# Two layers of a streaming encoder on one core: three tiles turned by a diagonal, one residual and the first ropes moved

## What is computed

```python
def trunk_layer(x, c, pos, w_ada, b_ada, g_pre, w_in, w_out, g_post, past):
    mod = jax.nn.silu(c) @ w_ada + b_ada
    shift, scale, gate = jnp.split(mod, 3, axis=-1)
    h = rms_norm(x, g_pre) * (1.0 + scale[:, None, :]) + shift[:, None, :]
    q_a, k_a, v_a, gate_a, q_i, k_i, w_i, q_b, k_b, v_b, gate_b = split_cols(h @ w_in)
    # rope on q_a, k_a, q_i, k_i, q_b, k_b
    o_a = dsa_attention(q_a, q_i, w_i, pos, k_all, v_all, ki_all)   # keys chosen by an index score, top 256
    o_b, s_new = retention(q_b, k_b, v_b, s0)
    o_b = head_group_norm(o_b).reshape(B, T, W_B).astype(x.dtype)
    mixed = jnp.concatenate([o_a * jax.nn.silu(gate_a), o_b * jax.nn.silu(gate_b)], axis=-1)
    y = rms_norm(mixed @ w_out, g_post)
    x = x + gate[:, None, :] * y
    return x, (k_a, v_a, k_i, s_new.astype(x.dtype))
```

## Time and profile before

| what | value |
|---|---|
| median of three runs | 1457.58 us (1457.34 to 1458.71) |
| the profiled execution | 1458.35 us |
| its span, first to last instruction | 1456.5 us |
| mean granted clock of TensorE | 0.992 of full speed |
| TensorE busy | 1391.7 us (96%) |
| VectorE busy | 1012.3 us (70%) |
| ScalarE busy | 790.7 us (54%) |
| GpSimd busy | 414.3 us (28%) |

### The profile page before, as it was taken

The page is one execution under the profiler, slowest core; times in us unless marked ns, Lnnn a source line. Parts: engine busy times, 40 slices in busy tenths (PEclk is TensorE's granted clock), DMA queues, the critical chain, the costliest instruction groups (busy, mean ns, idle before and its releaser), DMA issues.

```text
span 1456.5 us, 24555 instructions
## 1 busy us (share of the span) xinstructions
PE 1391.7 (96%) x7663; PEld 1064.9 (73%) x7663; DVE 1012.3 (70%) x2985; ACT 790.7 (54%) x1934; POOL 414.3 (28%) x378
## 2 busy tenths in 40 slices
PE   6989999999999999999997999999999999999996
PEld 2765777788887677668876577878788766766885
DVE  0586889999996555542397889999999655554125
ACT  2555666666315666664453566666631566666432
POOL 3750333433331011001387114433343200100100
PEclk9999999999999999999998999999999999999998
DMA  8734343212232112223252111211222211222324
GB/s 292 232 113 126 94 126 108 66 37 61 57 89 64 43 38 68 80 64 103 95 185 52 27 46 37 64 32 50 61 56 77 68 37 48 71 64 67 109 87 159
DMA packets 125190, 122.05 MB, mean 84 GB/s; under 512 B 33256, under 2 KB 94024, under 8 KB 125064
## 3 DMA queue, kind: packets, MB, share of 16 engines
q1 hardware_dynamic: 124608, 120.36, 27.6%
q10 hardware_dynamic: 456, 0.13, 0.0%
HBM read 93.55 MB, written 26.90 MB: 83 GB/s over the span
## 4 chain that ended last, share of the span: by engine, by line
PE 63%; DVE 27%; issue 4%; DMA 2%; ACT 2%; POOL 1%; DVEq 0%; ACTq 0%; SPq 0%; POOLq 0%
PE proj L969 12%; PE proj L970 12%; PE proj L972 11%; PE turn L948 10%; DVE U L1712 7%; PE logit L996 6%; PE out_bank L1023 5%; PE spare L996 2%; DVE U L1897 2%; DVE probsT_more L1785 1%; DVE probsT_more L1787 1%; DVE by_cos_sin L1656 1%; DVE turned L1667 1%; DVE by_cos_sin L1654 1%; PE spare L934 1%
## 5 line engine op out<-in xcount | busy, mean ns | idle before, releaser
L969 PE MATMUL proj<-w_hi,h_hi 128*128 128x512 f32 (+2 forms) x1440 | 576.8, 401 | 2.6 <-ACT U L1266 1.5
L970 PE MATMUL proj<-w_lo,h_hi 128*128 128x512 f32 (+2 forms) x1440 | 537.1, 373 | 0.0
L972 PE MATMUL proj<-w_hi,h_lo 128*128 128x512 f32 (+2 forms) x1280 | 479.2, 374 | 0.0
L1496 POOL TENSOR_TENSOR w_lo<-w_raw,w_hi 128x512 fp32r<-128x512 f32 (+2 forms) x160 | 203.0, 1269 | 761.5 <-ACT w_hi L1217 761.5
L969 PEld LDWEIGHTS proj<-w_hi,h_hi 128*128 128x128 f32 x1440 | 273.4, 190 | 52.9 <-issue 16.4
L970 PEld LDWEIGHTS proj<-w_lo,h_hi 128*128 128x128 f32 x1440 | 273.7, 190 | 31.0
L972 PEld LDWEIGHTS proj<-w_hi,h_lo 128*128 128x128 f32 x1280 | 241.7, 189 | 37.4
L1712 DVE TENSOR_SCALAR_CACHE_REDUCE U<-score,cand 128x384 bf16<-128x384 f32 x310 | 222.6, 752 | 2.2
L996 PE MATMUL logit<-keys,queries 64*128 64x512 f32 (+4 forms) x454 | 137.3, 542 | 3.3 <-ACT U L1352 2.9
L1332 ACT ACTIVATE probsT_more<-turn 128x512 f32<-128x512 f32 (+3 forms) x156 | 76.1, 490 | 96.1 <-PE turn L948 95.8
L948 PEld LDWEIGHTS turn<-ident,U 128*128 128x128 f32 x600 | 68.3, 141 | 52.0 <-issue 36.9
(11 more groups left out here) (195 smaller groups left out, 2156.6 us busy)
## 6 DMA issues: line engine op xcount, KB each, us to landing
w_raw<-in_w_in_dram SPq DMA_DIRECT2D x80, 256.0 KB, 3.2
probsT_more<-in_w_ada_dram SPq DMA_DIRECT2D x64, 256.0 KB, 4.0
score<-mixed_dram SPq DMA_DIRECT2D x36, 256.0 KB, 2.9
score<-in_w_ada_dram SPq DMA_DIRECT2D x32, 256.0 KB, 4.9
w_raw<-in_w_out_dram SPq DMA_DIRECT2D x32, 256.0 KB, 3.3
U<-in_x_prompt_dram SPq DMA_DIRECT2D x12, 512.0 KB, 4.1
mixed_dram<-U SPq DMA_DIRECT2D x24, 192.0 KB, 2.1
gates_dram<-U SPq DMA_DIRECT2D x18, 256.0 KB, 2.3
```

What stands on the lines that cost most here:

```text
L969: nc.tensor.matmul(out, h_hi[:, k, tile], hi, start=(k == 0), stop=False)
L970: ins = nc.tensor.matmul(out, h_hi[:, k, tile], lo, start=False, stop=(t == SAMPLE and k == KT - 1))
L972: ins = nc.tensor.matmul(out, h_lo[:, k, tile], hi, start=False, stop=(k == KT - 1))
L1496: nc.gpsimd.tensor_tensor(w_lo[:, s % WS, 0:w], w_raw[:, n % RAWS, 0:w], w_hi[:, s % WS, 0:w].bitcast(F32), ALU.subtract).then_inc(w_lo_re ...
```

## The change

Five things are done.

1. The second layer's tiles 6, 7 and 8 (`RAW_TILES`) are no longer scaled by GpSimd (`norm_x`) and turned by the identity, but turned raw with a diagonal, as in layer 0. The diagonals lie in `probs_last` and are made in steps 89, 90 and 91 (`raw_rows`). `mean_squares` for them goes.
2. The last residual of layer 0 (tile 8) moves from the end of step 89 to step 90, behind `rope` (`last_residual`). Its squares on ScalarE move behind `take_turn` of step 90.
3. In the first chunk of both layers `rope` comes first; the hidden tile is taken in halves, one behind `rope`, one behind the first index relus. In layer 0 that tile is the one formerly taken at the end of the step before.
4. The turned index queries and keys go into the out bank (ring `idx_turns`, one bank) and not into `turns`.
5. ScalarE's `split_hidden` in this chunk stands behind `take_turn`, ahead of the copy of the next projection; GpSimd's `lower_hidden` of layer 0 stands behind `lower_weights`.

The diff, cut to its core:

```diff
+RAW_TILES = [SAMPLE - 2, SAMPLE - 1, SAMPLE]
...
-        return l, t, 0, 2 if t >= XLAG and l + 1 < DEPTH else 1
-    for late in range(1, XLAG + 1):
-        if 0 < i - late and i < STEPS and lct(i - late)[1] == OUT1 and lct(i - late)[2] == SAMPLE:
-            return lct(i - late)[0], SAMPLE + late, 1, 2
+        return l, t, 0, 2 if t >= XLAG and t - XLAG not in RAW_TILES and l + 1 < DEPTH else 1
     return None
+
+
+def raw_rows(i):
+
+    for late in (0, 1, 2):
+        if 0 <= i - late < STEPS and i < STEPS and lct(i - late)[1:] == (OUT1, SAMPLE) and lct(i - late)[0] + 1 < DEPTH:
+            return lct(i - late)[0] + 1, RAW_TILES[late]
+    return None
+
+
+def last_residual(i):
+
+    return 0 < i < STEPS and lct(i)[1:] == (0, 0)
...
+        idx_turns = Ring([out_bank], IDX_TURN_AT, [idx_turned], [idx_turn_taken])
...
-            def turn_input(t):
-
-                pe.wait_ge(diagonal_ready, t + 1)
+            def turn_input(l, t):
+
+                pe.wait_ge(diagonal_ready, diagonal_ordinal(l, t) + 1)
...
-                        ins = nc.tensor.matmul(turns.bank(key)[:, b * P:(b + 1) * P], xt(t)[0:n, k * P:(k + 1) * P],
-                                               root_diagonal[0:n, t % 2, :], start=True, stop=True)
+                        ins = nc.tensor.matmul(turns.bank(key)[:, b * P:(b + 1) * P],
+                                               xt(l * NT + t)[0:n, k * P:(k + 1) * P], diagonal(l, t)[0:n, :],
+                                               start=True, stop=True)
...
             def turn_hidden(l, t):
-                if l == 0:
-                    turn_input(t)
+                if turned_raw(l, t):
+                    turn_input(l, t)
                     return
...
+                    if q == TURN_QUARTER and i >= 0 and kind(i) == "idx":
+                        for l, t in hidden_turns(i - 1):
+                            split_hidden(l, t)
+                    if q == TURN_QUARTER and last_residual(i):
+                        l = lct(i)[0] - 1
+                        act.wait_ge(x_new, l * NT + SAMPLE + 1)
+                        square_x(x_ordinal(l, SAMPLE))
...
-                    input_diagonal(input_rows(i))
-                for l, t in hidden_turns(i - 1):
-                    if l == 0:
-                        lower_hidden(l, t)
+                    input_diagonal(0, input_rows(i))
+                if raw_rows(i):
+                    input_diagonal(*raw_rows(i))
+                if i < 0:
+                    lower_hidden(0, 1)
                 if i + 1 < STEPS and weight_slice(i + 1) is not None:
                     lower_weights(weight_slice(i + 1))
+                for l, t in hidden_turns(i - 1):
+                    if l == 0 and i >= 0:
+                        lower_hidden(l, t)
...
                 for l, t in hidden_turns(i - 1):
-                    if l:
+                    if l and kind(i) != "idx":
                         take_hidden(l, t)
...
+                    if q == 0 and last_residual(i):
+                        add_residual(lct(i)[0] - 1, SAMPLE, unit)
+                    if i >= 0 and kind(i) == "idx" and q < 2:
+                        for l, t in hidden_turns(i - 1):
+                            take_hidden(l, t, (q,))
...
-                    if lo == 0:
+                    if not last_residual(i + 1):
                         add_residual(l, t, unit)
-                for l, t in hidden_turns(i):
-                    if l == 0:
-                        take_hidden(l, t)
```

More of the change, by code:

```diff
@@ L337 @@
 TURN_AT = {key: n for n, key in enumerate(TURNS)}
+IDX_TURN_AT = {("q", g): n for n, g in enumerate(k for k in range(STEPS) if kind(k) == "idx")}
 ATT_LOGITS = [key for key in LOGITS if key[0] == "l" and kind(key[1]) == "att"]
@@ L668, in xt, with turned_raw, diagonal_ordinal, diagonal @@
             return third_input if n < NT and x_slot(n) == 2 else xt_slots[x_slot(n)]
+        def turned_raw(l, t):
+            return l == 0 or t in RAW_TILES
+        def diagonal_ordinal(l, t):
+            return t if l == 0 else NT + (l - 1) * len(RAW_TILES) + RAW_TILES.index(t)
+        def diagonal(l, t):
+            return (late_diagonal if l else root_diagonal)[:, t % 2, :]
         def wait_x(eng, n):
@@ L942, in ada_columns, with turn @@
                 return ins
-            def turn(key, pieces):
-                turns.wait_free(pe, key)
+            def turn(key, pieces, ring=turns):
+                ring.wait_free(pe, key)
                 for n, piece in enumerate(pieces):
-                    ins = nc.tensor.transpose(turns.bank(key)[:, n * P:(n + 1) * P], piece, ident[:])
-                turns.filled(ins, key)
+                    ins = nc.tensor.transpose(ring.bank(key)[:, n * P:(n + 1) * P], piece, ident[:])
+                ring.filled(ins, key)
             def project(g, quarter):
@@ L1292, in take_turn @@
             def take_turn(g):
-                turns.wait_full(act, ("q", g))
-                src = turns.bank(("q", g))
+                ring = turns_of(g)
+                ring.wait_full(act, ("q", g))
+                src = ring.bank(("q", g))
                 if kind(g) == "ret":
@@ L1464, in _ @@
                 for l, t in hidden_turns(i - 1):
-                    if l:
+                    if kind(i) == "out":
                         split_hidden(l, t)
```

64 lines of the change are left out of this document (35 added, 29 removed).

## The result

The changed kernel takes 1465.49 us (median; 1464.41 to 1466.83), the kernel before 1457.82 in the same comparison (1457.34 to 1458.71): 1.0051 of its time, with a 95% interval of 1.0039 to 1.0063. It is slower by 7.7 us. The forecast was 1456.7 with a range to 1461.0, so the time lies outside, on the slow side, in the direction of rival (c) and 5 us beyond it.

A forecast was written before the change was run, and what follows sets the result against it. The prediction took TensorE's own work plus its waits as the bound, with 10.4 us of waits at steps 90 to 92 to win. It summed -5.6 + 3.4 + 1.3 = -0.9 us to 1456.7 us, range 1452.5 to 1461.0.

The forecast's parts named there:

- rival (c): Both first-chunk adaLN stalls lower the clock (+2.8), waits +4.2, second layer gains 4.0: +3.0 us, 1460.6 us; chance 0.22.
- Term three: First layer's first chunk: one clock drop counted behind the new TensorE stalls, the first being partly absorbed: +1.3 us.
- Term two: First layer's first chunk: adaLN turns at steps 4 and 6 wait for a bank: +3.4 us, floor +2.3, ceiling +4.5.
- The early lag of 0.8: First layer's steps 0 to 3: GpSimd's order and rope meeting its passes put TensorE 0.8 us behind.
- Term one: Second layer's first chunk: rope first shortens TensorE's waits at steps 90 to 92: -5.6 us, bounds -7 and -4.
- The bank at no cost: Moving the index turns into the out bank costs nothing, as nobody else writes it in this chunk.
- The shared port: Removing GpSimd's three scalings frees VectorE of 9.3 us by the rule, almost nothing by the trace; chance of rule 0.05.

The follow-up runs named there:

- filling the stalls: Changed kernel plus unused products (18 and 24) ahead of the adaLN stalls of steps 4 and 6: 1460.29 us, ratio 1.0017.
- the first of the three kernels with both repairs: Changed kernel with adaLN products in their step's third quarter and, in the second layer's first chunk, ScalarE's copy before splits and squares: 1450.16 us, ratio 0.9946.
- the second layer's part alone: Changed kernel with the first layer's first chunk in its old order, index turns keeping their own bank: 1453.29 us, ratio 0.9961.
- kernel without diagonals: Second layer's change alone, but tiles 6 to 8 scaled by GpSimd and turned by the identity: 1455.86 us, ratio 0.9991.
- first layer's part alone: Changed kernel with the second layer's tiles, last residual and order put back as before: 1471.00 us, ratio 1.0081.
- GpSimd in its old order: Changed kernel with the first layer's hidden tile lowered ahead of the weight slice again: 1468.71 us, ratio 1.0071.
- the kernel with the bank alone: Kernel before with only the turned index queries and keys moved to the out bank, in a ring of their own: 1456.32 us, ratio 0.9986.

## Why the prediction was wrong

The sum was -5.6 + 3.4 + 1.3 = -0.9 us; by the ledgers of the two profiles it is -3.2 + 6.6 + 5.0 = +8.4. Every term erred to the same side.

**Term three, the clock: the step that failed most.** I counted one drop and 1.3 us, because "the first is partly absorbed". TensorE lost 1.5 and 3.5 us behind the two stalls (1.7 and 5.0 not granted in the windows), and filling the stalls brought 5 back. Two mistakes are in it. A drop was priced from the 4 us of the earlier trace rows, and the second lasted through three windows of 4 us. And the waits that could absorb anything (2.6 us by my own count) had already been used up by the 3.6 us of lag from the wait itself: the first drop came on top, and the lag at step 5 was 2.58 where I had 1.1.

**Term two, the waits: the places right, the size half.** The two places, the bank and the chain that ends in it were as said, but the term measured 6.6 us against 3.4, beyond its own ceiling of 4.5. At step 4 the products were put at 84.7 and came at 84.22; 2.6 were to be absorbed by the next waits and 2.1 were. At step 6 they were put at 109.0 and came at 111.69. The copy of the rows was right within 0.6 us (predicted end 105.75, measured 106.29). What was missed is that `rope` waits for VectorE as well as for the copy: the relus of the step behind (2.88 and 1.19 us), held up by GpSimd's 2.95 us pass, end only at 107.8, and `rope` then took 2.5 us instead of 1.85. I had followed the operand and not the queue. Behind the second stall 1.1 us were to be absorbed; instead a wait of 0.9 for GpSimd came on top. The early lag of 0.8 was right in size, but it is not GpSimd's order that makes it: with the old order it was larger.

Rival (c) had both stalls, both drops and the second layer's gain at 4.0. With the measured 5.0 for its 2.8, 6.6 for its 4.2 and 3.2 for its 4.0 it gives 1466.0: it was the right story at too small prices.

**Term one, the second layer: 3.2 instead of 5.6 in the changed kernel.** The turn of step 90 came 7.2 us earlier, better than the 5.7 that I took, since the wait of 5.69 was what a low clock ahead of it had left of 7.2. Of these 7.2, 3.6 were given back by step 91. I had 1.8 and 0.3 for the bank of tile 5 and it was 2.72 (the residual's last instruction 1.77 beside a weight slice), 1.3 for `rope` of step 91 and it was 1.53. The rest is clock once more: the diagonal turns behind the 2.72 took 3.65 us, and 2.34 behind the same wait of 2.70 in the first of the three kernels with both repairs, whose clock stayed at 1.00. A drop into a new wait was in my lower bound of 4 but not in the sum. Alone, without the first layer's lag, the same part gave more (4.3 to 5.7, of which the bank is 1.6 to 2).

**The bank at no cost** was wrong by a gain of 1.6 to 2. I had looked for who else writes it and not for who stands behind whom in the ring that the keys left: the tile behind the adaLN products waited 1.44 us in the earlier trace rows for VectorE's taking of them, 0.28 after, and 0.45 in the second layer's part alone. That this is the whole of the gain is argued, not shown.

**The shared port.** The rows on which I chose against the rule held: in the kernel without diagonals, as before, a `rope` instruction beside the scaling takes 0.48 us. The Trainium skill, page "SBUF — State Buffer", section "SBUF: two separate sides", would have the instruction at 764.14 blocked until the scaling ends at 767.26; the trace does not agree. But I concluded that the scalings cost almost nothing, and that was wrong: putting them back, with the `means` that belong to them, costs 4.4 us. By the rows they act through the queues of GpSimd and VectorE. One reading of mine was too simple: the `rope` of 4.3 us in the earlier trace rows lay beside two passes of GpSimd, the one of 2.77 us and a weight slice of 1.52 us from 84.53.

**The range** was too narrow at the upper end because rival (c) was its edge. The clock's price, the least known number, stood in it as one value, and the waits stood in it at 4.2, under the ceiling that term two gave itself.

## What to carry to other kernels

Before an operation is put ahead of another on one engine, list who waits for the one that now comes later, down to small products at the head of a step: here two groups of eight instructions with two columns each stood where the loss of 12 us arose, and moving them half a step cured it. Price a new TensorE stall by its wait and by the clock behind it as separate terms, each with its own bounds; here the new waits at the two stalls were 6.4 us and the clock behind them 5.0. And when a wait has gone, look at what each engine does between the operand's arrival and the waiting operation (here ScalarE's splits and squares ahead of a copy, 3 us) before looking elsewhere.

## What the hardware showed

- A stall of 3.19 us was followed by 1.7 us not granted, and by 3.4 in the first layer's part alone. One of 4.20 had 5.0, its like of 4.19 there 5.1. One of 4.26 (GpSimd in its old order; 0.59 and 0.56 in the windows 86 to 90 and 90 to 94 us) had 3.4. TensorE was busy for the whole of the windows from 114 to 122 us, which stood at 0.50 and 0.75.
- A short wait can be followed by a low clock too: 1.01 us for the adaLN products of step 4 by 0.57 in the window 82 to 86 us in the kernel with the bank alone, and by 1.00 in the kernel before (1.00 us) and in the second layer's part alone (1.01 us), whose order there is the same.
- The same wait does not always have the same sequel: 1.91 us near 950 was followed by full clock in one kernel and by windows of 0.85 and 0.72 in another, whose code there is the same. This alone is worth 1.7 us (0.12%), and a difference of that size between two kernels' profiles should be looked for in the windows before it is put down to their orders.
